# Moving fourteen gathered expert rows out of the attention stage of a hybrid transformer layer

## The reference

```
h = rms_norm(x);  q, k, v, u_g, v_g = split(h @ w_in)              # 8 heads of 128, 8 gating groups of 128
y_sb = stick_breaking_attention(rms_norm(q), rms_norm(k), v)        # strictly causal, blocks of 128
y_sg = gelu(u_g) * (w_s @ rms_norm(gelu(v_g)) + b_s)                # per 128 positions
x = x + concat(rms_norm(y_sb), rms_norm(y_sg)) @ w_out
h2 = rms_norm(x);  q = rms_norm(h2 @ w_query)                       # per head, two halves of 128
v1, i1 = top_k(q[0] @ keys[0].T, 16);  v2, i2 = top_k(q[1] @ keys[1].T, 16)
top16 of the 256 sums v1 + v2  ->  8 heads x 16 experts of 16384, gate = softmax
x = x + sum over the 128 chosen of  gate * gelu(expert_u[i] . h2) * expert_v[i]
```

## The kernel before

| pieces | stage |
|---|---|
| 78 to 111 | input projection of tiles 1 to 3; tile 0's rows begin at 92 |
| between 111 and 112 | attention of tiles 1 to 3, head by head, with the gating beside it |
| 112 to 127 (`OUT_B`) | output projection of tiles 1 to 3 |
| 128 to 143 (`QUERY_B`) | their query projection |
| 144 to 215 (`AHEAD`) | up projections of the experts 0 to 71 x 128; beside 36 of them DVE retrieves the experts of the three tiles, then come five **batches** of six pieces in which the gates of 64 tokens each are spread and stored |
| 216 to 283 (`DOWN`) | down projections of those |
| 284 to 395 (`BOTH`) | the last mixed stage, up and down in turn |
| 396 to 399 | end |

## Time and profile before

### The profile page before, as it was taken

How to read it: one execution, slowest core, us unless ns; L and a number is a source line. 1 busy time by engine, 2 the same in 40 slices (tenths; PEclk the granted TensorE clock), 3 DMA queues, 4 the chain that set the end, 5 groups by cost and what they waited for, 6 DMA issues and landing times.

```text
span 3044.0 us, 43228 instructions
## 1 busy us (share of the span) xinstructions
PE 2892.1 (95%) x17829; PEld 2737.0 (90%) x17829; DVE 2197.6 (72%) x3102; ACT 1187.6 (39%) x1390; POOL 1543.4 (51%) x630
## 2 busy tenths in 40 slices
PE   7899899978989899999899999999999999999998
PEld 6677788866779899999899999999999999999998
DVE  6756476765677579998787577777677676776776
ACT  6755532457233233333343333333333333332331
POOL 0000263321332258882223588788876776766762
PEclk9999999989999999999999999999999999999999
DMA  9637538854796766776778899999999999998996
GB/s 362 262 144 286 206 130 341 342 209 180 274 361 233 275 230 228 245 243 239 273 270 333 339 357 362 359 367 360 352 368 350 402 361 357 366 366 341 371 375 219
DMA packets 183951, 916.04 MB, mean 301 GB/s; under 512 B 16945, under 2 KB 76449, under 8 KB 78273
## 3 DMA queue, kind: packets, MB, share of 16 engines
q1 hardware_dynamic: 115888, 485.79, 43.0%
q0 software_dynamic: 56112, 406.05, 34.9%
q10 hardware_dynamic: 11808, 22.29, 1.9%
HBM read 872.31 MB, written 41.68 MB: 300 GB/s over the span
## 4 chain that ended last, share of the span: by engine, by line
PE 69%; DVE 14%; DMA 8%; ACT 5%; issue 2%; POOL 2%; SPq 0%; DVEq 0%; ACTq 0%; POOLq 0%
PE ps L1624 11%; PE ps L1953 9%; PE ps L1955 9%; PE ps L1954 9%; PE ps L1884 6%; PE ps L1886 6%; PE ps L1885 6%; PE ps L1869 4%; PE ps L1611 3%; DVE ring_lo L1069 2%; PE ps L1927 2%; DVE rows L1296 2%; DMA rows<-peer_u_rows,idx_far 2%; DMA ring_raw<-w_query 2%; ACT ring_hi L663 2%
## 5 line engine op out<-in xcount | busy, mean ns | idle before, releaser
L588 POOL TENSOR_TENSOR ring_lo<-ring_raw,ring_hi 128x2048 fp32r<-128x2048 f32 x217 | 1054.5, 4860 | 725.6 <-ACT ring_hi L663 723.2
L663 ACT ACTIVATE ring_hi<-ring_raw 128x2048 fp32r<-128x2048 f32 x400 | 762.0, 1917 | 703.5 <-DMA ring_raw<-peer_u 230.0
L1884 PE MATMUL ps<-bT_hi,ring_hi 128*128 128x320 f32 x2048 | 644.4, 315 | 12.6 <-issue 6.9
L1953 PE MATMUL ps<-a_hi,ring_hi 128*128 128x320 f32 x2048 | 634.5, 310 | 5.1 <-DVE a_lo L1463 2.3
L1885 PE MATMUL ps<-bT_lo,ring_hi 128*128 128x320 f32 x2048 | 637.0, 311 | 0.0
L1886 PE MATMUL ps<-bT_hi,ring_lo 128*128 128x320 f32 x2048 | 636.6, 311 | 0.0
L1954 PE MATMUL ps<-a_lo,ring_hi 128*128 128x320 f32 x2048 | 633.5, 309 | 0.0
L1955 PE MATMUL ps<-a_hi,ring_lo 128*128 128x320 f32 x2048 | 633.5, 309 | 0.0
L1069 DVE TENSOR_TENSOR ring_lo<-ring_raw,ring_hi 128x2048 fp32r<-128x2048 f32 x183 | 420.3, 2313 | 234.7 <-ACT ring_hi L663 234.4
L616 POOL DMA_INDIRECT rows<-peer_u_rows,idx_far x128 | 219.7, 1716 | 474.0 <-DVE z_far L1296 436.6
L1884 PEld LDWEIGHTS ps<-bT_hi,ring_hi 128*128 128x128 f32 x2048 | 388.7, 190 | 13.7 <-issue 12.9
(11 more groups left out here) (290 smaller groups left out, 3709.4 us busy)
## 6 DMA issues: line engine op xcount, KB each, us to landing
ring_raw<-peer_u SPq DMA_DIRECT2D x128, 1024.0 KB
ring_raw<-peer_v SPq DMA_DIRECT2D x128, 1024.0 KB
ring_raw<-w_in SPq DMA_DIRECT2D x80, 1024.0 KB
ring_raw<-w_out SPq DMA_DIRECT2D x32, 1024.0 KB
ring_raw<-w_query SPq DMA_DIRECT2D x32, 1024.0 KB
g_pair<-gates_scratch SPq DMA_DIRECT2D x64, 320.0 KB
gelu_scratch<-ahead ACTq DMA_DIRECT2D x72, 160.0 KB
g_in<-gelu_scratch SPq DMA_DIRECT2D x72, 160.0 KB
```

Of the source, the lines that this page charges most:

```text
L588: pool.tensor_tensor(ring_lo[s][:], ring_raw[s][:], ring_hi[s][:].bitcast(F32), ALU.subtract)\
L663: act.activation(ring_hi[place(n)][:], ring_raw[place(n)][:], ACT.Copy).then_inc(hi_ok[SLOT[n]], 1)
L1884: pe.matmul(dst, hi[:, e], bT_hi[:, k, 0:NEAR], start=(k == 0), stop=False)
L1953: pe.matmul(dst, hi[:, col], a_hi[:, par, e, :], start=(e == 0), stop=False)
```

## The change

The rows beside the attention go: `ATTEND_ROWS` is all zeros. Eight of the fourteen are taken by the query projection of tiles 1 to 3, whose even pieces 128 to 142 get three rows for two. The other six fall to the last mixed stage, where `fill_rows` spreads what is left (164 rows for 158). Since the order of the rows is fixed, every row from the 36th on stands later in the program: eight to fourteen places of the list in the output projection, six from piece 143 to the end of the down projections.

```diff
-ATTEND_ROWS = (2, 2, 2, 2, 2, 2, 2, 0)
+ATTEND_ROWS = (0, 0, 0, 0, 0, 0, 0, 0)
...
     for n in range(OUT_B, AHEAD - 1):
-        ROWS_AT[n] = 0 if n == QUERY_B - 1 else 1 if n == QUERY_B - 2 or n % 4 == 3 and n < QUERY_B else 2
+        ROWS_AT[n] = 0 if n == QUERY_B - 1 else 1 if n == QUERY_B - 2 or n % 4 == 3 and n < QUERY_B else \
+            2 if n < QUERY_B or n % 2 else 3
```

## The result

The changed kernel took 3069.3 us, the median of four executions (3061.9 to 3086.5), against 3043.8 for the kernel before in the same set: ratio 1.0098, 95% interval 1.0057 to 1.0139. A second set of twelve executions of the unedited changed kernel (experiment 7) gave 3064.0 us and 1.0076 [1.0043, 1.0109]. So it is some 23 to 30 us slower, where the prediction summed up 11. The traced execution of the first set took 3086.5 us (its span is 3084.7), the slowest of its four; the traced execution of the second set took 3064.9 us (span 3063.2).

The account below looks back on a forecast made before the run. PE, busy 95% of the span, was taken as the bound, so only its waits count. Terms summed to +11.2 us on the profiled 3045.7, giving 3056.9; the median's 2.6 more gave 3059.5, predicted as 3059 us, range 3041 to 3078.

Parts of the forecast that it names:

- rivals that were to cost 7 to 16 us more: DMA engines full in the mixed stage (3075 us, chance 0.15); query loads at the output projection's rate (3067 us, 0.1).
- Attention, 0: Attention: removing 14 rows takes 32 us from DVE but gains 0, since ACT and PE's chain sets the pace.
- Start of the attention, -0.4: Attention start: fewer gathers ahead of the load of `sgnB`, 0.4 us gained; ends 0 and -4.3.
- End of the output projection, -0.2: Output projection's end: a gelu of 0.21 us leaves ACT's queue ahead of a square root and PE's transposes, -0.2 us.
- The gelu's table load, +1.5: Query projection: the moved gelu stands on PE's path and needs a table load of 1.28 us, +1.5 us in all.
- End of the query projection, +1.3: Query projection's end: ACT's square root waits for a table load, delaying PE and the retrieval 1.3 us; upper end +3.6.
- Query loads, +1: Query projection: eight more gathers slow the loads of pieces 133, 137 and 141, a third of a microsecond each.
- Batches, +7.0: Batches: rows shifted by six make each batch do what the one before did, +7.0 us; ends -2.3 and +8.8.
- The first rival: Batches: the turn from "u" to "v" costs no more than another "v" batch, -2.3 us, 3050 us in all; chance 0.15.
- Mixed stage, +1: Last mixed stage: six more rows raise the DMA rate from 377 to some 385 GB/s, +1 us; ends 0 and +17.
- the rival of full DMA engines: Mixed stage: DMA engines are full, so six rows more cost +17 us instead of +1, 3075 us; chance 0.15.
- the rival's own sign: Mixed stage: a load over 14.7 us makes `ring_lo` late for PE, deciding for full DMA engines (+17 us, chance 0.15).

Follow-up runs that it names:

- Experiment 8: Kernel before with six rows more beside the attention (20 for 14), so 152 rows in the mixed stage; ratio to before 1.0105 [1.0048, 1.0161].
- experiment 4: Kernel before with six rows fewer beside the attention (8 for 14), query projection kept at 30, mixed stage at 164; ratio to before 1.0050 [1.0024, 1.0076].
- experiment 11: Kernel before with six rows fewer beside the attention, 164 in the mixed stage, and row "out" moved from piece 307 to 308; ratio to before 1.0042 [1.0009, 1.0076].
- 12: Kernel before with six rows more ahead of the query projection (five in the input projection, one in the output projection), mixed stage 152; ratio 1.0053 [1.0022, 1.0085].
- experiment 3: Kernel before with six rows moved from the down projections to the last mixed stage (164 rows), nothing else changed; ratio to before 1.0060 [1.0035, 1.0085].
- 9: Changed kernel with row "out" moved from piece 307 to 308, both loads still issued at piece 307; 3044.7 us, ratio to before 1.0015 [0.9989, 1.0041].
- 10: Kernel before with row "out" moved from piece 304 to 303, mixed stage still 158 rows; ratio to before 1.0049 [1.0019, 1.0079].
- experiment 5: Changed kernel with the second row of piece 305 moved to 306, so the loads of "out" and "h" are issued at different pieces; ratio to before 1.0038 [1.0008, 1.0069].

## Why the prediction was right, and where it was not

The range and the sign of most steps held; the sum of 11 us was too small by 12 to 19. That the measured time lies in the range is in part luck. The range reached up to 3078 us for the sake of rivals that were to cost 7 to 16 us more in other ways, and two errors partly cancel: the query projection was 8 us better than its terms and the mixed stage 14 us or more worse.

- **Attention, 0: right.** Head period 11.67 us, and over all traces the time from piece 112 to 115 is 154.3 to 160.0 us without rows (six traces, mean 157.5) and 154.5 to 160.2 with fourteen at the old place (four, mean 157.1). It was right to price the removed rows at nothing. Experiment 8 shows that the stage isn't free for more rows, but for another reason than DVE's time: the third row's gather.
- **Start of the attention, -0.4:** `sgnB` took 6.67 us for 8.28, 1.6 us less where I had allowed 0.8, and was issued 0.87 us earlier; head 1's first step came 2.35 us earlier. That is inside the ends, more than I took; the mean over the traces shows none of it.
- **End of the output projection, -0.2:** too small to be seen.
- **The gelu's table load, +1.5: right**, 1.45 us. Both new loads are of 1.28 us with the function 0.01 us behind, as in the earlier trace rows. By the Trainium skill, page "ScalarE: Activation LUTs", section "What ACT_TABLE_LOAD costs", a drain of some 1.38 us should be added to each; the trace doesn't agree.
- **End of the query projection, +1.3: right.** ACT's square root starts 2.88 us after its copies of the scores (1091.89 to 1094.77) where it was 1.45 us (1099.00 to 1100.45), behind a table load, and from piece 144 to 150 the changed kernel took 1.5 us more (56.2 for 54.7). Over the traces that stretch scatters by more than this (53.2 to 61.9 us in the old placement, 55.6 to 56.2 in the new).
- **Query loads, +1 with ends 0 and +8.5: wrong, in sign.** The loads of pieces 133, 137 and 141 took 10.1, 9.6 and 9.4 us before and 9.5, 8.7 and 4.9 after (9.3, 6.9 and 7.7 in the second trace of the changed kernel). From piece 128 to 150 four traces of the old placement have a mean of 243.9 us and five of the new one 239.5: -4.4 where the terms summed to +3.8. I counted what the gathers add and not when they are issued. A load took some 5 us where hardly a gather moved beside it and 9 to 10 where gathers had most of the engines. That a row more moved DVE and so POOL's issues from ahead of the load to behind it is what I take from this; no run shows it by itself. Experiments 4, 11, 8 and 12, with 30 rows like the kernel before but shifted by six either way, took 228 to 234 us. So a gain should have been among the ends. Which of the rows' places decides it isn't settled: experiment 3, whose rows up to piece 216 stand as before, has loads of 9.8, 5.3 and 7.5 us there, so one and the same placement also differs from one execution to the next.
- **Batches, +7.0: right, by its mechanism.** Intervals 65.4, 65.4, 67.8, 56.8, forecast 65.4, 65.4, 67.7, 56.6. The same holds in the seven traces shifted by +6 (184 to 216: 327.6 to 331.6), the five unshifted (321.7 to 325.6) and the two shifted by -6 (314.9 and 315.4). The first rival (the turn from "u" to "v" costs nothing in its new place) falls.
- **Mixed stage, +1: the step that failed.** As priced (six rows, DMA rate) it was right: the rest is 811 to 826 us with 158 rows (mean of five 816.1) and 811 to 830 with 164 (mean of seven 816.5), and experiment 11 moves 384 GB/s with PE never idle, at a share of 0.98. So the rival of full DMA engines falls as a cost of the whole stage, +17. What was put at nothing is the turn: the six rows carry "out" from piece 304 to 307. That cost 15.7 and 14.8 us in the two traces of the changed kernel, in two parts. Some 9 us are POOL's wait for the store of tile 0's output, 8.2 us long, which now stands ahead of a piece of its own (310) instead of one of DVE's (307); experiments 9 and 10 show this part. The other 6 to 7 us are piece 309, whose load took 19.4 and 18.3 us (9.2 before) with the DMA engines full. Here the rival's own sign, a load of over 14.7 us, did come at one place, and so did the sign that I had named for being wrong, PE standing several times for `ring_lo`; experiment 5 takes this part away, but the wait then lasted 15.55 us and the whole turn still cost 12.9. The wait stood in the trace of before, and the rule of `lo_on_pool` in the code; I had asked of each moved row what it costs where it goes, but not of the one row that makes POOL wait.

Summed by stages the change is -4.4 + 6 or 7 + 14 to 16, some +17 us; twelve executions say +23 [13, 33], the first four +30 [17, 42]. The first interval holds it and the second ends there; what the 6 us or more between the sum and the measurements are is not shown. The first trace is longer still, by losses of which the second trace has few (experiment 7).

## What to carry to other kernels

When a list of work is shifted in a fixed program, look for the few items on it that make a queue wait for a transfer (a store that must land, a first use of a buffer), and ask what stands behind each in its new place; here they cost 15 us where all the rows that were merely moved cost some 2 net. Here a load took 5 or 9 us by what moved beside it, and the edit that added gathers won 4 us: the range of such a term needs both signs. Where stages repeat in fixed steps, a shift by a whole step can be read off the trace by moving the intervals along, to a fraction of a microsecond.

## What the runs showed of the hardware

**PE stops at the head of a loop when its instructions are fetched again.** The stops counted above stand only at every sixteenth piece, the head of PE's loop, and their number goes with what the instruction queue moves. That queue between 2290 and 2990 us (packets, MB, share): kernel before, two stops; experiment 4, five stops; experiment 5, none. In all fourteen traces it is 1 packet with no stop, 9 with one, 17 to 19 with two and 44 with five.

```profile
q8 instruction: 18, 0.29, 0.2%
```

```profile
q8 instruction: 44, 0.72, 0.4%
```

```profile
q8 instruction: 1, 0.02, 0.0%
```

So some passes through the loop need their instructions loaded anew and others none, and each pass that does costs 4.6 to 9.0 us at its head. It came 0 to 5 times in six, once with nothing edited in another place than before (experiment 7). Five such passes for none are some 33 us (experiment 4), so they may be a good part of the scatter between executions of one kernel, 41 to 56 us in the sets of the kernel before; only one execution of each set has a trace, so that isn't shown.

**A wait costs more than it lasts.** After PE's stop of 2.90 us at 2536.5 us in the kernel before, the granted clock was 0.50 (1.2 GHz) for the next 3 us, and 1.00 (2.4 GHz) ahead of it (columns as above):

```profile
2525.00:2533.00 8.00, 8.00 (x57) 8.00 (x56) 6.14 (x9) 2.80 (x4) 6.37 (x4) 1.00 1.00 379
2536.60:2539.60 3.00, 3.00 (x12) 3.00 (x13) 1.93 (x2) 0.00 (x0) 2.83 (x3) 0.50 1.05 410
```

Twelve matmuls in 3 us for some 21. So that stop cost 4.6 us, and the waits of 5.05 and 6.60 us at pieces 309 and 310, behind which the changed kernel's trace has the lower clock too, cost 6.65 and 9.02.
